# A two-layer trunk step on one core: the border to the dense feed-forward crossed by token tiles, modulation panels spread differently

## What is computed

```python
def adaln(cvec, w, b):
    return jnp.split(jax.nn.silu(cvec) @ w + b, 6, axis=-1)

def sublayer(x, shift, scale, gate, g_pre, g_post, fn):
    h = rmsnorm(x, g_pre) * (1 + scale[:, None]) + shift[:, None]
    out, aux = fn(h)
    return x + gate[:, None] * rmsnorm(out, g_post), aux

def swiglu(x, w1, w3, w2):
    return (jax.nn.silu(x @ w1) * (x @ w3)) @ w2
...
    bias = jnp.where(valid[None, None, :, :, None, :], bias, NEG_INF).reshape(H, rows, ncb, NA_COLS, nw)
...
            y_s, _ = sublayer(y_s, ms[0], ms[1], ms[2], g[0], g[1],
                              lambda h: even_mixer_latent(h, cache_a_k[:, e], cache_a_v[:, e], cache_b_k[:, e],
                                                          cache_b_v[:, e], b_rpb[e], *ew))
...
            ffn = lambda h: (swiglu(h, ff_w1[e], ff_w3[e], ff_w2[e]), None)
...
        y_p, _ = sublayer(y_p, mp[3], mp[4], mp[5], g[2], g[3], ffn)
        y_s, _ = sublayer(y_s, ms[3], ms[4], ms[5], g[2], g[3], ffn)
```

## Time and profile before

| | us |
|---|---|
| median of 3 runs | 1445.4 |
| lowest and highest | 1442.62, 1448.0 |
| the profiled execution | 1442.48 |
| its span in the trace | 1440.9 |
| mean granted clock of TensorE, of full speed | 0.984 |

### The profile page before, as it was taken

How to read it: one execution, slowest core, us unless ns; L and a number is a source line. 1 busy time by engine, 2 the same in 40 slices (tenths; PEclk the granted TensorE clock), 3 DMA queues, 4 the chain that set the end, 5 groups by cost and what they waited for, 6 DMA issues and landing times.

```text
span 1440.9 us, 18579 instructions
## 1 busy us (share of the span) xinstructions
PE 1349.9 (94%) x7178; PEld 1060.7 (74%) x7178; DVE 870.9 (60%) x1168; ACT 738.9 (51%) x961; POOL 98.8 (7%) x170
## 2 busy tenths in 40 slices
PE   7999789899999998999989899999999998899996
PEld 3997347799998877987557776667877734688884
DVE  2534676533334436789675795456966603979796
ACT  3532466622223326596264576445865403768674
POOL 0402420000000000200000200001000000000001
PEclk9999899999999999999999999999999999999998
DMA  9933997633343323323862698658997799999993
GB/s 352 306 137 120 362 372 278 212 117 117 125 149 135 108 97 117 122 83 117 295 246 107 264 400 302 231 209 298 401 324 283 264 399 409 410 384 407 377 375 132
DMA packets 132235, 358.17 MB, mean 249 GB/s; under 512 B 6236, under 2 KB 30200, under 8 KB 132024
## 3 DMA queue, kind: packets, MB, share of 16 engines
q1 hardware_dynamic: 120440, 321.53, 60.9%
q0 software_dynamic: 9344, 32.26, 6.5%
q10 hardware_dynamic: 2368, 3.23, 0.6%
HBM read 335.35 MB, written 22.55 MB: 248 GB/s over the span
## 4 chain that ended last, share of the span: by engine, by line
PE 76%; DVE 10%; DMA 5%; ACT 4%; issue 2%; POOL 2%; SPq 1%; POOLq 0%; DVEq 0%; ACTq 0%
PE bank L2313 30%; PE bank L1964 12%; PE bank L1719 7%; PE bank L1975 6%; PE bank L2261 6%; PE bank L1769 4%; PE bank L1716 3%; DMA ring<-in_moe_w_dram 2%; DMA arena<-shear 1%; DMA ring<-in_mod_w_dram 1%; DVE arena L2767 1%; DVE ring_parts L2468 1%; PE bank L2201 1%; DVE ring_parts L3007 1%; POOL arena L866 1%
## 5 line engine op out<-in xcount | busy, mean ns | idle before, releaser
L2313 PE MATMUL bank<-arena_parts 128*128 128x512 f32 x1072 | 263.3, 392 | 4.7 <-ACT arena_parts L1463 2.6
L3007 DVE TENSOR_TENSOR ring_parts<-ring,arena_parts 128x2048 fp32r<-128x2048 f32 x85 | 192.4, 2286 | 79.5 <-PE bank L2261 43.9
L2313 PEld LDWEIGHTS bank<-arena_parts 128*128 128x128 f32 x1072 | 199.3, 188 | 54.5 <-issue 11.6
L1463 ACT ACTIVATE arena_parts<-ring 128x2048 fp32r<-128x2048 f32 x85 | 161.6, 1917 | 29.7 <-DMA ring<-in_moe_w_dram 24.0
L2313 PE MATMUL bank<-ring_parts,arena_parts 128*128 128x512 f32 x504 | 135.2, 390 | 2.9 <-DVE ring_parts L3007 2.9
L1964 PE MATMUL bank<-ht_parts,arena_parts 128*128 128x384 f32 x352 | 118.3, 336 | 0.9 <-DVE xn_parts L2479 0.8
L1964 PE MATMUL bank<-ht_parts,ring_parts 128*128 128x384 f32 x352 | 117.6, 334 | 0.0
L1964 PE MATMUL bank<-xn_parts,arena_parts 128*128 128x384 f32 x352 | 117.6, 334 | 0.0
L2313 PEld LDWEIGHTS bank<-ring_parts,arena_parts 128*128 128x128 f32 x504 | 94.4, 188 | 23.8 <-DVE ring_parts L3007 4.2
L2702 DVE TENSOR_TENSOR arena<-arena,bank 128x384 f32<-128x384 f32 x22 | 12.2, 554 | 123.6 <-PE bank L1964 123.6
L1719 PE MATMUL bank<-ht_parts,ring_parts 128*128 128x384 f32 x256 | 85.7, 335 | 0.0
(11 more groups left out here) (501 smaller groups left out, 2635.6 us busy)
## 6 DMA issues: line engine op xcount, KB each, us to landing
ring<-in_moe_w_dram SPq DMA_DIRECT2D x144, 1024.0 KB, 7.1
ring<-in_mod_w_dram SPq DMA_DIRECT2D x24, 2048.0 KB, 12.4
arena<-in_moe_w_dram SPq DMA_DIRECT2D x48, 1024.0 KB, 7.0
ring<-in_ff_w_dram SPq DMA_DIRECT2D x23, 1024.0 KB, 7.8
ring<-in_w_in_odd_dram SPq DMA_DIRECT2D x6, 2048.0 KB, 8.5
ring<-in_w_in_even_dram SPq DMA_DIRECT2D x5, 2048.0 KB, 10.8
ring<-in_ff_w_dram SPq DMA_DIRECT2D x5, 2048.0 KB, 7.8
routed<-cst POOLq DMA_DIRECT2D x1, 7168.0 KB, 23.4
```

The costliest lines, as they stand in the source:

```text
L1463: act.activation(whi_moe[high_at(w, n_)], e_half(j, h), ACT.Copy).then_inc(whi_ready, 1)
L2313: ins = pe.matmul(bank[base + b][:, :], lhs[:, c_, :], rhs[:, k, 512 * b:512 * b + 512], start=(first and h == 0 and k == 0 and n_ == 0), ...
L3007: dve.tensor_tensor(e_half(j, h, low=True), e_half(j, h), whi_moe[high_at(w, 2 * j + h)], ALU.subtract).then_inc(wlo_ready, 1)
```

## The change

It has six parts.

1. Modulation panels 4 to 11 go before units 0, 3, 6, 9, 12, 14, 16 and 18; their copy, fold and addition before the end of the loop (ACT at unit 21, TensorE at 22, DVE at 23). Panels 12 to 15 form a group of their own in bank 3 and are multiplied in the up stage behind column blocks 3, 5, 7 and 9, folded at block 12. There they use ring slot 2, and the up panels alternate between slots 0 and 1. A load waits for the panel before it in its own slot.
2. The scratch tensor `shear` is first filled with the negative number, then 21 small DMAs copy only the valid windows. The 64 `affine_select` are gone; DVE waits for the DMAs.
3. POOL's zero fill waits for `up_done` 4 (block 3 of the feed-forward) instead of `ot_dve` 4.
4. The border by token tiles: tile 0 is turned inside `out_proj(0, 1)`, tile 1 inside `out_proj(0, 2)`, tile 2 behind the part of column block 0 that needs tiles 0 and 1 only. Block 0 is thus done in a part of 256 token columns and one of 128. ACT modulates a tile and DVE splits it right after its norm (`modulate_tile`, `tile_halves`).
5. The gate rows' matmuls go behind `turn_tile(2)`, into bank 0; ACT copies the rows of the gate before (`keep_gate(0, 1)`) later, behind the first sum of squares.
6. The first down panel is split before the last silu and product, and TensorE's own wait for the last product is gone.

The core of the diff (the last two pieces are TensorE's and ACT's streams):

```diff
         def panel_slot(i):
-            return (2, 0, 2, 0)[i] if i < 4 else i % RING
+            return slots_[i]
...
-        panels += [mod_panel(m) for m in range(4, 16)]
+        panels += [mod_panel(m) for m in range(4, 12)]
         panels += [(("out0", j), [("k512", cut(I["w_out_even"][0], 512 * j, 512))]) for j in range(2)]
...
+        for j in range(KF // 2):
+            panels.append((("up", j), [("lo256", cut(I["ff_w1"][0], 256 * j, 256)),
+                                       ("hi256", cut(I["ff_w3"][0], 256 * j, 256))]))
+            m = 12 if j == 1 else 10 + j
+            if j == 1 or 3 <= j < 6:
+                panels.append(mod_panel(m))
...
+        slots_ += [2 if key[0] == "mod" else 1 - key[1] % 2 for key, _ in panels[20:35]]
...
-            return 4 + i // 2 if i % 2 == 0 and i < 24 else None
+            return {0: 4, 3: 5, 6: 6, 9: 7, 12: 8, 14: 9, 16: 10, 18: 11}.get(i)
...
-                sp_.wait_ge(*released(i - RING))
+                sp_.wait_ge(*released(before_in_slot(i)))
...
-            for k_ in range(7):
-                pool.dma_start(shear[:, :, k_, :],
...
+            pool.dma_start(shear.rearrange("h c r k -> (h c r k)").rearrange("(p n c) -> p n c", p=P, c=256),
+                          barred.unsqueeze(1).to_broadcast([P, 7, 256])).then_inc(bias_in, 16)
+            pool.wait_ge(bias_in, 16)
+            for c0_, n_, step, at_, at_step in ((0, 8, -1, 0, 0), (8, 49, 0, 0, 1), (57, 7, -1, 48, 0)):
+                row = 7 * GRID_W
+                for k_ in range(7):
+                    pool.dma_start(bass.AP(tensor=shear.tensor, offset=c0_ * row + k_ * GRID_W + at_,
+                                           ap=[[GRID_W * row, B_HEADS], [row + at_step, n_], [1, 16]]),
...
-                for qh in range(16):
-                    then(pool.affine_select(out=lo[:, qh], in_=lo[:, qh], compare_op=ALU.is_ge, fill=NEG,
...
-            pool.wait_ge(ot_dve, 4)
+            pool.wait_ge(up_done, 4)
             for dst in (routed[:, :], answered[OVER_AT - 2 * P:N_SLOTS, :]):
...
+            def turn_tile(t):
+                pe.wait_ge(xn_ready, 3 + t + 1)
+                for b in range(2):
+                    for k in range(4 * b, 4 * b + 4):
+                        ins = pe.transpose(bank[2 * t + b][:, P * (k % 4):P * (k % 4) + P], xnk[:, k, t, :], ident)
+                    ins.then_inc(xn_turned, 1)
...
+                        if m == 0 and (t, 4 * j + n) in ((1, 4), (2, 5)):
+                            turn_tile(t - 1)
...
-            gate_row(1, 0)
-            for k in range(KD):
-                turn_in(1, k)
+            panel(("up", 0))
+            for g in range(2):
+                up(0, g, 0, 2 * P)
+            turn_tile(2)
+            pe.wait_ge(v_ready, tile_part(1, 0, 1))
+            gate_row(1, 0)
...
+                    up(f, g, 0 if f else 2 * P, T).then_inc((gate_done, up_done)[g], 1)
+                if f in (3, 5, 7, 9):
+                    mod_mm(12 + (f - 3) // 2)
+                if f == 12:
+                    mod_turn(G_DENSE)
             pe.wait_ge(gb_kept, 4)
-            pe.wait_ge(prod_ready, KF)
...
-            keep_gate(0, 1)
             split_up(0)
             norm_tiles(0)
             keep_gate(1, 0)
-            for k in range(KD):
-                modulated(1, k)
             split_up(1)
             for f in range(KF):
+                if f == KF - 1:
+                    split_down(0)
```

More of the change, by code:

```diff
@@ L1085, in norm_tiles @@
             def norm_tiles(s):
+                if s == 0:
+                    for t in range(NT):
+                        root_of_product(0, t)
+                        if t == 0:
+                            keep_gate(0, 1)
+                        root_of_sum(0, t)
+                        modulate_tile(t)
+                    return
                 root_of_product(s, 0)
@@ L2691, in _ @@
             norm_tiles(0)
-            for k in range(KD):
-                halves_of(1, k)
             split_up(1)
@@ L2728, in _ @@
                .then_inc(soft_abs, 1)
-            split_down(0)
             split_down(1)
```

153 lines of the change are left out of this document (91 added, 62 removed).

## The result

| | us |
|---|---|
| changed kernel, median of 6 runs (lowest, highest) | 1454.94 (1453.5, 1456.85) |
| kernel before, median of 6 runs beside it | 1446.28 (1442.62, 1448.2) |
| ratio, 95% interval | 1.0061 (1.0045 to 1.0076) |
| span of the changed kernel's profiled execution | 1453.2 |

The change made the kernel slower, by 0.6%, 8.7 us. The forecast was +14.1, 1459.5 with a range from 1432 to 1468: the right side, the right mechanism, and a size that was too large. Beside the 1454.94 of the median, the forecast alone had 1453 to 1466.

The account below looks back on a forecast made before the run. TensorE's work plus its gaps was taken to bound the kernel. The terms -12.6 -1.5 -0.4 +8.4 -5.1 +23.5 +1.8 made +14.1 us on a median of 1445.4, so 1459.5, range 1432 to 1468.

Parts of the forecast that it names:

- the forecast alone: Whole kernel: the summed terms without the rivals, 1459.5 us, with bounds giving 1453 to 1466; chance 0.52.
- Attention loop and tail: Attention: panels spread over later units gain 12.6 us; fewer panels and no fold behind unit 18 gain 1.5.
- Border: Out-projection to feed-forward: turning token tiles early starts block 1 at 283.1 against 283.5, gain 0.4 us, at worst 2.8 lost.
- Panels in the up stage: Feed-forward: four panels at 1.85 us and a fold of 1.0 where TensorE is never idle, loss 8.4.
- Down border: Before the down-projection: splitting the first panel early removes a 3.60 us gap and 1.4 of colder clock, gain 5.1.
- The stall: Up stage: the late zero fill delays modulation panel 13, so TensorE waits 23.5 us, plus 1.8 of colder clock.
- The rule of sharing: DMA engines: queues take turns record by record, equal counts whatever the size (fill 4 KB, up panel 1 KB, modulation panel 2 KB).
- the head start: Up panel 3: SP's data come after 1.5 us, POOL's fill after 3.0, so 32 records per engine pass alone.
- Two signs of being wrong: A wait near 314 under 10 us refutes the queue-sharing reading; an out-projection start later than 213 refutes the loop sum.
- Rival 2: Up stage: larger turns for short records, so the fill bites less: stall 9.8 us, 1.6 of clock, 1445.6; chance 0.18.
- Rival 1: Up stage: the fill does not bite, panel 13 lands before t+18.5, no stall: sum -11.2, 1434.2 us; chance 0.22.
- Rival 3: Attention: DVE may bound the loop, which then gives 5.6 us less, stall as forecast: 1465.1 or 1467.9; chance 0.08.

Follow-up runs that it names:

- panels_back: fill_early with modulation panels 4 to 15 before every even unit of the attention loop again, as in the kernel before: 1438.61 us, ratio 0.9945.
- nine_tiles: fill_early with a ninth modulation panel (12) in the attention loop before unit 20, only 13 to 15 in the up stage: 1434.47 us, ratio 0.9921.
- fill_early: The changed kernel with POOL's zero fill released at its old place (ot_dve 4, before the out-projection), nothing else different: 1436.91 us, ratio 0.9926.
- fill_block2: The changed kernel with the zero fill released one block earlier (up_done 3): 1457.84 us, ratio 1.0070.
- fill_1k: The changed kernel with the late zero fill written from a source row of 1 KB instead of 2 KB: 1454.13 us, ratio 1.0047.
- b_fill_late: The kernel before with only the zero fill moved to up_done 4: 1446.61 us, ratio 0.9997.

## Why the prediction came out as it did

**What bounds the kernel** held: every microsecond of the table above is TensorE's work or its gaps.

**Attention loop and tail**, -12.6 and -1.5: measured -13.9. The chain of landings 5.45 us apart held (unit 18's panel at 185.30, 1.6 of it the later opening). The masks' share is 1.9 by panels_back; I had left them inside the sum.

**Border**, -0.4: the trace of the change has -1.6, the old border put back gives 0 in the median. The out-projection became 2.8 us longer (3.2 forecast), and block 1 followed its end, 253.87, by 15.7 us and not 16.5, mostly because ACT's eight modulations of tile 2 took 2.90 us where I had 3.56. The 128-column matmuls cost 0.113 each (47 starts from 263.09 to 268.42), so the choice of 0.122 against 0.1734 was the right one. What I did not have is the clock behind it, 1.6 us in this trace and nothing in those of panels_back and nine_tiles.

**Panels in the up stage**, +8.4: 9.1, and 1.6 of clock that belongs to the border. I took the 1.85 of attention, where the next instruction overlaps; between matmuls of 384 columns it is 2.05.

**Down border**, -5.1: 3.75 in the trace, 7.0 by the medians (5.5 to 10.4). The two do not agree, and that stays open.

**The stall**, +25.3 with its clock: this term was mis-sized. Measured are 8.67 and 4.52 us of waits and 1.72 and 1.67 of cold matmuls, 16.6 (with 9.1 for the panels, 1.6 of clock and the gap's -3.6 that is 23.7 of the row's 24.5), and by the medians of the changed kernel and fill_early 18.0. The rule of sharing, one record each whatever its length, is what the windows from 307 us on show. The step that failed is the head start: "so 32 records of the up panel pass alone". I let POOL's data come 3.0 us after its wait ended and SP's 1.5. In the trace the wait ended at about 298.0, SP's first records come just after 299 and the fill's take until 305 to appear: 75, 310, 380, 375, 333 and 283 records of the up panel pass from 299 to 305, 1756 of its 2048, some 110 of 128 per engine. With 18 rounds at 0.222 and 64 at 0.261 from 305 on, panel 13 would be there at 325.7; its matmuls started at 325.47. So the same arithmetic with 18 rounds in place of 96 gives the measured landing. In fill_block2, where the fill runs first, the same arithmetic gave 20 and the trace 18.49. The second wait, 4.52 us for panel 14, was left out of the forecast: the fill, which in my count would have been almost done when panel 13 landed, had some 2090 of its 2848 records to go at 316.8, when up panel 4 was issued, and that panel and panel 14 shared the engines with it. So two errors partly cancel: 6.2 of the 16.6 us come from a wait that the forecast did not have, and that the size came out as near as it did owes something to luck. Two signs of being wrong had been named. The wait came in under 10 us, which was to mean that the reading of how the queues share is wrong; the reading held, and the sign had left out the head start. The out-projection started at 213.39, later than 213, but the opening was 1.6 us later in this trace, and the sum for the loop held.

**The rivals.** Rival 2, that the fill bites less, gave 9.8 us of stall and 1445.6, and its number for panel 13 lies nearer than mine. Its mechanism is refuted: turns do not grow longer for short records, since 407 and 408 of them stand side by side at 1 KB and 4 KB. The same rows bear on the rule of the Trainium skill, DMA: Bandwidth & Descriptors, "Queues, rings and completion order", that an engine takes a whole packet of several descriptors from each queue in turn: over 5 us the counts of records are equal. The page of the profile calls its records packets, and if each is one, that is what the rule gives; how many descriptors are in one no run here shows. What failed is the working that took the source rows for descriptors: a third of the bandwidth for an up panel is not what it got (0.42 of 2.07 MB, a fifth). Rival 1 was the danger that I had seen rightly and put at 0.22: the head start on which it rested was real, and nearly four times as long as I had it (just after 299 to 305, against 1.5). Rival 3 fell: the loop gave its 13.9 us. Behind unit 18 TensorE does wait for DVE, 1.57 and 0.87 us, and a ninth panel fitted there at no cost.

## What to carry to other kernels

A background transfer costs by what is urgent beside it. Count the records of the urgent queue that are still to come once both run, give each the background queue's record time on top, and compare with the slack of that load's consumer. Here loads that were issued only two blocks before their use, and bulk traffic in the same stretch, each caused no wait alone and cost 18 us together, so judge such moves in pairs. And put bulk writes where the weight queue is waiting for slots: in fill_early the fill ran alone from 218 to 250 us beside the out-projection, and TensorE waited for no panel.

## What was not expected of the hardware

- A queue that starts while another keeps the engines full gets its first records late: the fill about 5 us after its issue (299.65, first records between 304.5 and 305; 6 us in fill_1k and b_fill_late) instead of 2 (issued at 228.22, first records after 230 before the change), the up panel in fill_block2 more than 4 us instead of 1. So whoever comes first keeps the engines for some 3 us more.
- The software queue's records stay near 4 KB (2848 and 2944 for 11.53 MB) with source rows of 2 KB, of 1 KB, and with destination pieces of 1 KB that do not touch.
- The granted clock of one and the same stretch differs between executions. At the start of block 1, behind the same 128-column matmuls and waits of 0.65 and 0.89 us, it was 0.72 over 5 us in the changed kernel and 1.00 in nine_tiles, and this was worth about 1.6 us.
